# Three of eight expert blocks with 64 tokens and two matmul passes per weight in place of three, experts placed by load

## The reference

```python
def swiglu(x, w_gate, w_up, w_down):
    return (jax.nn.silu(x @ w_gate) * (x @ w_up)) @ w_down

def moe_ffn(x, w_router, w_gate, w_up, w_down):
    ...
    logits = (xt @ w_router).astype(F32)
    top_val, top_idx = lax.top_k(logits, TOP_K)
    top_w = jax.nn.softmax(top_val, axis=-1)
    ...
    yp = lax.map(run, (xp.reshape(n_blocks, MOE_BLOCK, D), block_e)).reshape(P, D)
    contrib = yp[dest] * w_s[:, None].astype(x.dtype)
    out = jnp.zeros((T, D), x.dtype).at[tok_s].add(contrib)
    return out.reshape(B, L, D)
```

## Time and profile before

| | us |
|---|---|
| median of three runs | 1415.78 |
| lowest and highest of them | 1414.43, 1418.35 |
| the profiled execution, its own time | 1414.72 |
| its span, from first to last instruction | 1412.9 |

### The profile page before, as it was taken

One profiled execution on the slowest core, in us unless ns is written; L12 is line 12 of the kernel. 1 busy time (PEld: TensorE's weight loads), 2 busy tenths in 40 slices (PEclk: granted clock), 3 DMA queues, 4 the chain that ended last, 5 costly groups with the idle time before them and its releaser, 6 DMA issues.

```text
span 1412.9 us, 18929 instructions
## 1 busy us (share of the span) xinstructions
PE 1367.8 (97%) x6511; PEld 1027.0 (73%) x6511; DVE 1146.6 (81%) x1212; ACT 862.2 (61%) x927; POOL 69.3 (5%) x62
## 2 busy tenths in 40 slices
PE   6999989999998999899999999999999999999998
PEld 3887768888887877678667776777767767777666
DVE  5989786644549888866998889889898898888988
ACT  4344635444335455536777767777777777776775
POOL 0020011000000110100220000000000000000300
PEclk9999999999999999999999999999999999999999
DMA  7443234965483344144999989989899899898996
GB/s 287 173 179 140 99 109 166 395 249 190 170 331 120 149 149 179 46 155 150 386 376 369 422 306 414 409 307 424 343 374 408 308 423 392 325 424 305 411 406 234
DMA packets 63878, 395.71 MB, mean 280 GB/s; under 512 B 7186, under 2 KB 7758, under 8 KB 23898
## 3 DMA queue, kind: packets, MB, share of 16 engines
q1 hardware_dynamic: 58858, 375.64, 68.6%
q10 hardware_dynamic: 3104, 12.58, 2.2%
q0 software_dynamic: 1872, 6.90, 1.4%
HBM read 376.22 MB, written 18.87 MB: 280 GB/s over the span
## 4 chain that ended last, share of the span: by engine, by line
PE 85%; DVE 9%; issue 2%; ACT 2%; DMA 1%; POOL 0%; SPq 0%; DVEq 0%; ACTq 0%
PE bank L1470 20%; PE bank L1471 19%; PE bank L1745 19%; PE bank L1722 12%; PE bank L1517 5%; DVE w_lo L971 3%; PE bank L1512 2%; PE bank L1623 1%; PE bank L1483 1%; PE bank L1732 1%; DVE ys L960 1%; DMA raw<-in_moe 1%; ACT w_hi L660 1%; PE bank L1616 1%; DVE tmp L960 1%
## 5 line engine op out<-in xcount | busy, mean ns | idle before, releaser
L971 DVE TENSOR_TENSOR w_lo<-raw,w_hi 128x2048 fp32r<-128x2048 f32 (+2 forms) x383 | 797.4, 2092 | 128.6 <-ACT w_hi L660 125.5
L660 ACT ACTIVATE w_hi<-raw 128x2048 fp32r<-128x2048 f32 (+2 forms) x383 | 670.3, 1756 | 170.0 <-PE bank L1745 63.8
L1470 PE MATMUL bank<-w_hi,hT_hi 128*96 128x512 f32 (+3 forms) x1232 | 487.9, 396 | 3.0 <-DVE hT_lo L1332 1.4
L1471 PE MATMUL bank<-w_hi,hT_lo 128*96 128x512 f32 (+3 forms) x1232 | 478.3, 388 | 0.0
L1470 PEld LDWEIGHTS bank<-w_hi,hT_hi 128*96 128x96 f32 (+1 forms) x1232 | 213.5, 173 | 68.1 <-issue 7.8
L1471 PEld LDWEIGHTS bank<-w_hi,hT_lo 128*96 128x96 f32 (+1 forms) x1232 | 213.7, 173 | 60.0 <-issue 1.0
L1722 PE MATMUL bank<-w_lo,hT_hi 128*96 128x512 f32 (+3 forms) x880 | 232.9, 387 | 0.0
L1722 PEld LDWEIGHTS bank<-w_lo,hT_hi 128*96 128x96 f32 (+1 forms) x880 | 145.6, 167 | 52.3 <-DVE w_lo L971 2.6
L1745 PE MATMUL bank<-w_hi,act_lo 128*96 128x512 f32 (+1 forms) x420 | 113.4, 394 | 2.4 <-DVE act_lo L1309 2.4
L1745 PE MATMUL bank<-w_hi,act_hi 128*96 128x512 f32 (+1 forms) x420 | 113.0, 393 | 0.8 <-ACT act_hi L854 0.8
L1745 PE MATMUL bank<-w_lo,act_hi 128*96 128x512 f32 (+1 forms) x420 | 112.3, 391 | 0.0
(11 more groups left out here) (231 smaller groups left out, 997.4 us busy)
## 6 DMA issues: line engine op xcount, KB each, us to landing
raw<-in_moe SPq DMA_DIRECT2D x224, 1024.0 KB, 9.5
raw<-in_mix SPq DMA_DIRECT2D x56, 1024.0 KB, 4.8
raw<-in_dense SPq DMA_DIRECT2D x28, 1024.0 KB, 4.9
raw<-in_moe SPq DMA_DIRECT2D x43, 512.0 KB, 3.5
raw<-in_moe SPq DMA_DIRECT2D x16, 768.0 KB, 7.8
slot_h<-x_squared ACTq DMA_DIRECT2D x1, 6144.0 KB, 43.8
slot_y<-x_squared ACTq DMA_DIRECT2D x1, 6144.0 KB, 17.9
slot_y<-y SPq DMA_DIRECT2D x8, 384.0 KB, 11.1
```

The lines of the kernel that those rows point to most:

```text
L660: nc.scalar.activation(HI[:, split_slot, 0:width], RAW[:, raw_slot, 0:width], ACT.Copy)\
L971: vec.tensor_tensor(LO[:, split_slot, 0:width], RAW[:, raw_slot, 0:width], HI[:, split_slot, 0:width].bitcast(F32), ALU.subtract).then_inc ...
L1470: mm(out_, left[0], right[0], start=start, stop=False)
L1471: mm(out_, left[1], right[1], start=False, stop=False)
```

## The change

Expert 0 stays block 0, with 96 places. Experts 1 to 7 are ranked by their number of tokens on the chip (`router_blocks`, new, on VectorE after the first chunk of block 0). The four with most tokens become the heavy blocks 1, 3, 5, 7 with 96 places, the three with fewest the light blocks 2, 4, 6 with LCAP = 64. What doesn't fit goes to further blocks, as before. SyncE reads the number of the expert for each block from `nbe`.

In a light block the 64 tokens' high parts and their low parts lie side by side as one stationary operand of 128 columns (`hT_hi`, and `act_hi` for the activation). Each slab needs two passes, `w_hi` and `w_lo`, over this operand. Rows 0 to 63 of the bank then hold the high part's product, rows 64 to 127 the low part's. ScalarE copies the lower half to `lo_sum` (`lo_copy`), and one matmul with a swapped identity (`add_lo`) adds it to the upper half, before SiLU. The low part times the low weight, left out before, comes in this way. For the down product the two halves are added once per block: `y_lo` is copied by ScalarE and VectorE, and the next heavy block adds it with two matmuls behind its second slab (`add_y_lo`); its `take_y` waits for them.

The core of the diff:

```diff
+LCAP = 64
+LIGHT = 3
+PAIR = CAP + LCAP
...
+    def router_blocks(dve, v, tt, ts, stt):
+        tt(key[:, :], total, key_row, ALU.add)
+        other = key[:, :].unsqueeze(1).broadcast_to([P, NE, NE])
+        own = key[:, :].unsqueeze(2).broadcast_to([P, NE, NE])
+        tt(cmp[:, 0, :, :], other, own, ALU.is_gt)
+        tt(cmp2[:, 0, :, :], other, own, ALU.is_equal)
...
+        reduce(rank[:, :], cmp[:, 0, :, :])
+        ts(light[:, :], rank[:, :], float(NE - LIGHT), None, ALU.is_ge)
...
 # SyncE
-                with sp.Fori(0, NE) as b:
-                    block_slabs(sp.snap(FFN_SLABS * b + first), bass.ds(b, 1), b)
+                block_slabs(of(0), slice(0, 1), 0, (0, CAP), (2 * CAP, CAP))
                 sp.wait_ge(sem("experts_known"), 1)
+                for i in range(LIGHT):
+                    heavy = 2 * CAP + PAIR * i
+                    block_slabs(of(2 * i + 1), expert(2 * i + 1), 2 * i + 1, (heavy - (LCAP if i else CAP), LCAP if i else CAP),
+                                (heavy + CAP, LCAP))
+                    block_slabs(of(2 * i + 2), expert(2 * i + 2), 2 * i + 2, (heavy, CAP), (heavy + PAIR, CAP))
...
 # ScalarE, one chunk of a light block
+                    turned_hi_light(q - 1)
+                    ffn_split(p + 3, n0, r0, width)
+                    lo_copy(n0 + p + 1, parity)
+                    ffn_split(p + 4, n0, r0, width)
+                    silu_light(q, k, parity)
+                    ffn_split(p + 5, n0, r0)
 # ScalarE and VectorE, take_y in a heavy block behind a light one
+                        act.wait_ge(sem("y_lo_added"), y_added)
 # VectorE, one chunk of a light block, and block 0
+                    ffn_split(p + 3, n0, width)
+                    mult_light(q, parity)
+                    ffn_split(p + 4, n0, width)
+                    turned_lo_light(q)
+                    ffn_split(p + 5, n0)
...
                     chunk(4, qb + 1, 1, n0)
+                    router_blocks(dve, v, tt, ts, stt)
+                    chunk(7, qb + 2, 0, n0)
                     router_places(dve, v, tt, ts, stt)
-                    chunk(7, qb + 2, 0, n0)
 # TensorE
+            def gate_up_light(n, s, k0, nk, width, parity):
+                pe.wait_ge(hi_ready, n + 1)
+                for k in range(nk):
+                    w_hi, _ = w_parts(s, k * 2 * width, (k + 1) * 2 * width)
+                    mm(PS[parity][:, 0:2 * width], HTH[:, k0 + k, 0:2 * LCAP], w_hi, start=k0 + k == 0, stop=False)
+                pe.wait_ge(lo_ready, n + 1)
+                for k in range(nk):
+                    _, w_lo = w_parts(s, k * 2 * width, (k + 1) * 2 * width)
+                    ins = mm(PS[parity][:, 0:2 * width], HTH[:, k0 + k, 0:2 * LCAP], w_lo, start=False, stop=k0 + k == KD - 1)
+            def add_lo(k, parity, width=CHUNK):
+                pe.wait_ge(sem("lo_copied"), k + 1)
+                mm(PS[parity][:, 0:2 * width], R["swap"][:, :], LO_SUM[:, 0:2 * width],
+                   start=False, stop=True, skip_group_check=True).then_inc(sem("lo_added"), 1)
...
+                        gate_up_light(n0 + p, slot(p), 0, 4, CHUNK, 1 - j)
+                        if opening:
+                            add_lo(k0, 0)
+                        else:
+                            turn_act_light(q - 1)
+                        gate_up_light(n0 + p + 1, slot(p + 1), 4, 4, CHUNK, 1 - j)
...
+                        down_light(n0 + p + 2, slot(p + 2), q - 1, opening)
+                        add_lo(k0 + 1 + j, 1 - j)
...
+                with pe.Fori(0, LIGHT) as i:
+                    ffn_block(pe.snap(2 * i + 1), True, y_ready=2 * i + 2)
+                    light_block(pe.snap(2 * i + 2), i)
```

345 lines of the change are left out of this document (278 added, 67 removed).

## The result

The changed kernel takes 1409.64 us in the median of seven runs (1406.62 to 1412.66), the kernel before beside it 1416.58 us (1414.43 to 1418.35). The ratio is 0.995, with a 95% interval of 0.9937 to 0.9964: faster by 7 us, where 22 were forecast, and just outside the range of 1382 to 1409. The profiled execution has a span of 1406.1 us, 6.8 less than before.

A forecast was written before the change was run, and what follows sets the result against it. TensorE, busy 97% of the span, was taken as the bound, with VectorE and the DMA next in light blocks. Terms: -27.3 (light blocks) + 2.5 (block 0) + 2.8 (heavy blocks) = -22.0 us, a median of 1394 us, range 1382 to 1409.

The forecast's parts named there:

- the rival's 1493 us: Light blocks: TensorE at its lower clock throughout adds 52 us a block, kernel 1493 us; chance of the clock 0.06.
- +2.5: Block 0: router work between VectorE's splits makes TensorE wait 3.7 us for act_lo against 1.2 before, +2.5 us.
- the +2.8: Heavy blocks 1, 3, 5, 7: two more matmuls, which take_y waits for, cost 0.7 x 4 = 2.8 us (1.8 to 10.6).
- the 82 to 84 us: VectorE in a light block: 82.9 us of work plus up to 1 us of waiting at the block's end.
- So a light block is 84 us: Light blocks 2, 4, 6: VectorE and DMA limits set 84 us in place of 93.1, saving 9.1 each, 27.3 in all.
- full buffers, not a limit: DMA at a block's end: the dip to 237 GB/s was put to full buffers and not counted as a limit.
- The first: Light blocks: the loop through four engines adds 0.4 to 0.6 us a chunk, block 88 to 90 us, kernel 1400 to 1411; chance 0.17.
- The sign and the order of the chances: Whole kernel: faster 0.82, same 0.08, slower 0.10.
- 0.60: Whole kernel: the chance given to the forecast of 1385 to 1401 us, with light blocks of 84 us.

The follow-up runs named there:

- half splits: Changed kernel, but ScalarE and VectorE split only the left half of each slab's columns in light blocks, loads whole: 1400.09 us, ratio 0.9878.
- The run with a smaller store: Changed kernel, but in light blocks a slab is loaded when the one five before it is split, not six: 1417.62 us, ratio 1.0001.
- the run without the copy: Changed kernel, but in light blocks ScalarE doesn't copy the bank's lower half and TensorE doesn't add it: 1408.71 us, ratio 0.9939.
- the one with half the bytes: Changed kernel, but in light blocks only the left half of each slab's columns is loaded, splits and matmuls whole: 1397.38 us, ratio 0.9862.

## Why the prediction was wrong

**What held.** The direction; eight blocks, of which three light; TensorE no longer the limit; the clock, where the rival's 1493 us stayed far; the heavy blocks 1 and 5 at +0.9 and +0.7 (0.7 forecast); block 0 at +2.4 (+2.5), near the forecast in each wait. Block 7 was 0.4 us shorter and block 3, which began at the lower clock, 1.7 longer, so that the sum of the heavy ones fits the +2.8 in part by luck. For VectorE the 82 to 84 us fit the 83.9 with the DMA relieved, but luck is in that too: its busy time was put at 82.9 us with up to 1 us of waiting, and it was busy for 79.5 and idle for 4.9 of 84.4 us in block 4.

**The step that failed** is "So a light block is 84 us. VectorE says 82 to 84, the DMA 81 to 84". It was mis-sized by 4.2 us, times three. The later of two limits was taken for the whole block:

1. The DMA's 84.0 us are 34.5 MB at the 411 GB/s of the earlier trace rows throughout, and the lower rate at a block's end was set aside as "full buffers, not a limit". The rate was right: 410 GB/s for 75 us. So were, in two blocks of three, the 84.0 us for a DMA that nothing hinders: 84.0 and 84.5 with half splits, and 87.2 in block 2, which is most of the 1.2 us that the mean of 85.2 lies above the forecast. The holes around the side transfers were in the rate already, both of them; TensorE, busy throughout, hid them in the kernel before:

```profile
856.00:861.00 5.00, 5.00 (x23) 3.26 (x22) 5.00 (x5) 3.76 (x3) 0.00 (x0) 1.00 1.00 368
...
906.00:911.00 5.00, 5.00 (x23) 3.52 (x22) 4.22 (x5) 4.29 (x4) 0.00 (x0) 1.00 1.02 360
```

2. What was missing is the end of the block. There VectorE, with small slabs and its side work, is the late one, the slots stay full, and the DMA moves 301 GB/s over 12 us and not 411. VectorE can't make up for it before, since it waits for slabs there. So limits of 85.2 and 83.9 us give 88.2, 3.0 more than the later one. The prediction said that limits which alternate "rarely give the better of the two", and then took a value that both reach singly; it even expected the end to give something back. The run with a smaller store shows that the store between the two counts, and the earlier trace rows had the ingredients: a DMA that is at its rate for 65 us and idles in part at the block's end, and a VectorE with its side work in that end.

A smaller part: the saving was taken from 93.1 us, and the three blocks lasted 92.6 before, which makes 1.6 us in all. The +1.1 us ahead of block 0 can't be put down to the change: in the profiled executions of this study block 0 began between 658.2 and 661.8 us, and in the kernel before at 659.4.

Of what the profile was to show, three things came out otherwise without a cost of their own: TensorE busy for 74.5 to 75.3 us in a light block (65 to 68 forecast; the recorded length of a matmul has its way through the array in it), the DMA at 391 to 395 GB/s (above 400), and VectorE busy for 90 to 91% of the time (above 95%).

**The rivals.** The first gave the right number (88 to 90 us; by the prediction's own prices a kernel of 1406 to 1412 us, not of 1400 to 1411) for the wrong reason; its mechanism is refuted by the run without the copy and the one with half the bytes. The sign and the order of the chances were sound, but 0.60 on a light block at the edge of both limits was too much.

## What to carry to other kernels

When a stage loses its main limit and the next two lie within a few per cent, its time can be more than either. Lay both out along the stage: where one of them is late in one part and the other in another, the parts add up. Relieve each alone to learn both limits, and make the store between them smaller by one to see whether they are coupled. A small transfer in a saturated stream can cost more than its bytes: read the hole that it leaves in the rate, and put it where the stream has slack. A number that fits a rival proves nothing until the cost it names is taken out.
